# Head norms of a hybrid decoder trunk: squares split into a rounded high part and a remainder for the sum over a head

## The chip, the cores and the metric

The kernel runs on one core of one Trainium2 chip. The metric is device time in microseconds (us) of one execution. The profile is that of one profiled execution of the same kernel. In it PE is TensorE (matrix products; PEld its weight loads), DVE is VectorE, ACT is ScalarE, POOL is GpSimd and SP is SyncE, which issues transfers.

## The reference

Two layers of a decoder trunk, for 256 prompt tokens and 8 x 8 sample tokens (320 in all), width 2048. Each layer takes an RMS norm, one wide input projection, three token mixers (A: sliding-window attention, B: causal pooling, C: gated linear attention), gates, a branch projection, a merge and an output projection. The change is in branch A, in the norm of each query and key head:

```
def rms_norm(x, g):
    xf = x.astype(jnp.float32)
    y = xf * lax.rsqrt(jnp.mean(xf * xf, axis=-1, keepdims=True) + EPS)
    return (y * g.astype(jnp.float32)).astype(x.dtype)
...
    q = rope(rms_norm(a_q.reshape(bsz, L, A_HEADS, A_HEAD_DIM), q_norm_g), pos)
    k = rope(rms_norm(a_k.reshape(bsz, L, A_KV_HEADS, A_HEAD_DIM), k_norm_g), pos)
```

There are 16 query heads and 4 key heads of 64 numbers. With 64 numbers a head, 128 partitions hold two heads, and a tile of 128 x 2 x 320 holds four heads of all 320 tokens: one such tile for the keys (k_norm), four for the queries (q_norm 0 to 3), in each of the two layers.

## The kernel before, in words

Everything is held transposed: channels in partitions, the 320 tokens along the free dimension. The weights stream in from memory in blocks of 128 x 1024 float32, one block a "beat". Each block is split into a rounded high part `w_hi` (ACT, `split_hi`, L1108) and a remainder `w_lo` (DVE, `split_lo`, L449), both float32r, and PE forms three products for each 128 x 128 piece: high by high, high by low, low by high (`block_products`, through `mm`, L1554). That is 24 main products of 320 columns in a beat. There are 5 buffers of raw blocks and 3 of high parts, so ACT and DVE run up to a few beats ahead of PE, and are held back by `half_used`, which PE raises after each half block.

The other work on PE (norms, attention, linear attention) is cut into side steps. `side_steps` assigns each of them a beat, and PE does a beat's side steps behind the main products of that beat. ACT and DVE each have a list of their own, written out by beat too, and each engine goes through its list in order: in the loop over beats DVE does `split_lo_to(Q + 2)`, then, in beats with scores, `vector_softmax`, `split_lo_to(Q + 3)` and `vector_probs`, then `vector_part`, then `rope_end`. ACT does `split_hi_to(Q + 2)`, in beats with scores `split_hi_to(Q + 3)`, then `scalar_part`. Semaphores (`act_done`, `vec_done`, `step_done` and others) carry the dependences; a `mark` notes the value that a later `wait_mark` waits for.

A head norm runs like this. DVE takes the projected tile from the accumulators into `ta` (L518). ACT squares it into `tc` (L1353), for k_norm in beat 70 and for q_norm k in beat 77 + 4k. PE, at the end of beat 72 or 79 + 4k, multiplies `tc` by `head_ones`, a float32 block of ones for each head, which leaves each head's sum of squares in `side` banks 2 and 3. ACT takes the inverse root (L1128, L1130) into `tb`; DVE's `rope_pair` (L468, L792) scales and begins the rotation; SP exchanges halves by transfers (`turned<-normed`); DVE's `rope_end` ends the rotation, in beats 75, 81, 86, 90 and 94.

Scores step j stands on PE at the end of beat 82 + 4j for j of 0 to 2, and later for the others; `p_turn` two beats behind it and `pv` three. So in beats 82, 86 and 90 `scored_at` is true. `prompt_softmax` waits for the scores step of that beat, `prompt_probs` for the exponentials that ACT forms from it (L1279, L1281), and ends with four scalings of the probabilities (L837, L838).

The step on PE before:

```
elif name in ("k_norm", "q_norm"):
    wm("head_squares", l, (name, k))
    for t in range(2):
        last = mm(side[:, 2 + t, 0:TOK], head_ones, tc[:, t, :])
```

Of the kernel before, what the change touches and what calls it, by code (L numbers as in the profile page):

```python
# [17 lines left out]
F32 = mybir.dt.float32  # L18
F32R = mybir.dt.float32r
BF16 = mybir.dt.bfloat16  # L20
U8 = mybir.dt.uint8
ALU = mybir.AluOpType
ACT = mybir.ActivationFunctionType
AX = mybir.AxisListType

P = 128
# [7 lines left out]
TOK = SEQ + SMP  # L34
# [15 lines left out]
G_CQ, G_CK, G_CV, G_U, G_BZ, G_K, G_V, G_Q, G_CZ, G_AZ = 0, 2, 4, 8, 12, 16, 17, 18, 22, 26  # L50
# [103 lines left out]
STEP_NO = {s: i for i, s in enumerate(ORDER)}  # L154
N_STEPS = len(ORDER)

ROPE_END = {75: ("k_norm", 0), 81: ("q_norm", 0)}
ROPE_END.update({82 + 4 * k: ("q_norm", k) for k in range(1, 4)})

# [25 lines left out]
def gated_at(beat, stage):  # L185


    wait = {G_AZ: 2}
    return [g for g in GATED if TAKE[g] + wait.get(g, 0) + stage == beat and g != GATED[-1]]
# [16 lines left out]
def trunk(nc, ins, outs):  # L206
    with ExitStack() as ctx:
        def sem(name):
            return ctx.enter_context(nc.semaphore(name))
# [3 lines left out]
        def place(name, shape, dt=F32, at=None):  # L213

            size = {F32: 4, F32R: 4, BF16: 2, U8: 1}[dt]
            for s in shape[1:]:
                size *= s
            if at is None:
                at = top[0]
                top[0] += -(-size // 64) * 64  # L220
            return nc.alloc_sbuf_tensor_at(name, shape, dt, offset=at)
# [8 lines left out]
        T1 = TOK * 4  # L230

        part_b, part_c, part_a = br0, br0 + 16 * T1, br0 + 32 * T1
# [14 lines left out]
        near_mask = place("near_mask", [P, NEAR, 32], U8)  # L247
        par = place("par", [P, DEPTH, R_END])
        ones = place("ones", [P, P])
        eps = place("eps", [P, 1])  # L250
        rstd = place("rstd", [P, TOK])
        ta0 = top[0]
        ta = place("ta", [P, 2, TOK])
        tb = place("tb", [P, 2, TOK])
        tc = place("tc", [P, 2, TOK])
# [38 lines left out]
        v_stack = [place("v_stack0", [P, 1024], F32R), place("v_stack1", [P, 1024], F32R, at=att0)]  # L294
        squares = place("squares", [P, 4, TOK], at=part_c)
        w_gate = place("w_gate", [P, GH * DK], at=part_c + 12288 + 6144)
        turned = place("turned", [P, 2, TOK], at=part_c + 10 * T1)
        normed = place("normed", [P, 2, TOK], at=part_c + 12 * T1)
        cq = place("cq", [P, GH, TOK], at=part_a)
# [11 lines left out]
        side = ctx.enter_context(nc.psum_tensor("side", [P, 4, 512], F32))  # L311
# [18 lines left out]
        level_k = sem("level_k")  # L330
        softplus_done = sem("softplus_done")
        swapped = sem("swapped")
        params_in = sem("params_in")
        rms_done = sem("rms_done")
        x_hi_ready = sem("x_hi_ready")
# [18 lines left out]
        marks = {}  # L354

        def wait_mark(e, *key):
            s, v = marks[key]
            e.wait_ge(s, v)
# [31 lines left out]
        head_ones = const[:, C_BLOCK:C_BLOCK + P]  # L390
# [34 lines left out]
        def _(dve):  # L425
            v = Counted(dve, vec_done)
# [464 lines left out]
            def vector_part(l, beat):  # L891

                if l == 0:
                    for j in squares_at(beat):
                        first_squares(j)
                if l == 0 and beat == 10:
                    dve.wait_ge(consts_in, 64)
                    v(dve.tensor_copy(gmask[:, :, :], gmask_f[:, NEAR:8, :]))
                    for j in range(4):
                        rows = slice(32 * j, 32 * j + 32)  # L900
                        v(dve.tensor_copy(near_mask[rows, :, :], gmask_f[rows, 0:NEAR, rows]))
                    v(dve.memset(q_s[:, :, :, :, :, :].rearrange("p i b j g t -> p (i b j g t)"), 0.0))
                    v.mark("masks", 0, 0)
                if beat == RMS_BEAT:
                    from_act()
                if beat == LR_AT + 1:
                    for i in range(2 if l else 0):
                        dve.wait_ge(y_out[i], 64 * l)
                    dve.wait_ge(half_used, last_half(l, beat))
                    dve.tensor_tensor(ta[:, 0, :], group_psum(GROUPS * l + LR_GROUP)[:, 0, :], rstd[:, :],  # L910
                                      ALU.mult).then_inc(main_free, 1)
                    marks[("lr", l, 0)] = (main_free, GROUPS * l + LR_GROUP + 1)
                if beat == 12:
                    log_decay_sum(l)
                if beat == 13:
                    decay_scan(l)
                if beat == 15:
                    clear_scores(l)
                if beat == 14:

                    v(dve.memset(lev_k[:, :, :], 0.0))
                    v.mark("keys_clear", l, 0)
                for g in gated_at(beat, 2):
                    gate_low(l, g)
                for g in gated_at(beat, 1):
                    gate_product(l, g)
                if TAKEN_AT.get(beat, G_CZ) < G_CZ:
                    take(l, TAKEN_AT[beat])
                for gi in range(4):
                    if beat == TAKE[G_U + gi] + 1:  # L930
                        pool_diff(l, gi)
                for k in range(1, 8):
                    if beat == 17 + 2 * k:
                        level_prep(l, k)
                    if beat == 18 + 2 * k:
                        level_scale(l, k)
                for name, k, _ in STEPS.get(beat, ()):
                    if name == "gate":
                        log_decay(l)
                    elif name == "level":  # L940
                        (near_take if k < NEAR else level_take)(l, k)
                    elif name == "pool":
                        wait_step(l, "pool", k)
                        for t in range(2):
                            v(dve.tensor_scalar(o_ab[:, 2 * k + t, :], side[:, 2 + t, 0:TOK],
                                                col(l, R_PS + 2 * k + t), None, ALU.mult))
                        v.settle()
                        v.mark("pooled", l, k)
                    elif name == "second_chunk":
                        second_state(l)  # L950
                    elif name == "sample_gla":
                        sample_state(l, k)
                    elif name == "gla_norm":
                        gla_scale(l, k)
                    elif name in ("k_norm", "q_norm"):
                        rope_pair(l, name, k)
                if TAKEN_AT.get(beat, 0) >= G_CZ:

                    take(l, TAKEN_AT[beat])
                if beat == TAKE[GATED[-1]]:  # L960
                    gate_product(l, GATED[-1])
                    gate_low(l, GATED[-1])
                if beat == 34:
                    carry_prep(l)
                if beat == 36:
                    carry_end(l)
                if beat in STACK_AT:
                    stack_low(l, STACK_AT.index(beat))
                for k in range(8):
                    if beat == (SAMPLE_AT[k - 1] if k else 51):  # L970
                        sample_sel(l, k)
                if beat in (50, SAMPLE_AT[GH - 1]):
                    sample_queries(l, int(beat != 50))
                if beat in (68, 70):

                    from_act()
                    v(dve.tensor_tensor(squares[:, 0:4:2, :], squares[:, 0:4:2, :], squares[:, 1:4:2, :], ALU.add))
                    v.mark("squares", l, (beat - 68) // 2)
# [88 lines left out]
        def _(act):  # L1067
            a = Counted(act, act_done)
# [127 lines left out]
            def scalar_part(l, beat):  # L1196
# [119 lines left out]
                if beat in STACK_AT:  # L1316
                    n = STACK_AT.index(beat)
# [25 lines left out]
                for k in range(2):  # L1343
                    if beat == 68 + 2 * k:
# [1 line left out]
                        if k:  # L1346
                            wait_step(l, "gla_norm", 0)
                        give(act.activation(squares[:, :, :], o_c[:, 4 * k:4 * k + 4, :], ACT.Square))
                for name, k, at in [("k_norm", 0, 70)] + [("q_norm", k, 77 + 4 * k) for k in range(4)]:
                    if beat == at:  # L1350
                        s, n = marks[("taken", l, G_K if name == "k_norm" else G_Q + k)]
                        act.wait_ge(s, n)
                        a(act.activation(tc[:, :, :], ta[:, :, :], ACT.Square))  # L1353
                        a.mark("head_squares", l, (name, k))

            def mix_pair(l, j):
                Q0 = BEATS * l + IN_BEATS + 18 * j
# [157 lines left out]
        def _(pe):  # L1515
# [37 lines left out]
            def mm(out, lhsT, rhs, start=True, stop=True):  # L1553
                return pe.matmul(out, lhsT, rhs, start=start, stop=stop)  # L1554
# [31 lines left out]
            def side_step(l, name, k, banks):  # L1586
# [104 lines left out]
                    for i in range(2):  # L1691
                        last = mm(side[:, i, 0:TOK], ones[:, :], squares[:, 2 * i, :])
                elif name in ("k_norm", "q_norm"):
                    wm("head_squares", l, (name, k))
                    for t in range(2):
                        last = mm(side[:, 2 + t, 0:TOK], head_ones, tc[:, t, :])
                elif name == "kv_turn":
                    wm("taken", l, G_V)
                    for t in range(2):
# [247 lines left out]
```

## Time and profile before

| what | us |
|---|---|
| median of 3 runs | 2290.7 |
| lowest and highest of them | 2290.34, 2290.79 |
| the profiled execution, its own time | 2289.56 |
| its span, first to last instruction | 2287.8 |
| PE busy in the span | 2280.6 |
| DVE busy | 1357.3 |
| ACT busy | 968.9 |
| POOL busy | 70.8 |

The granted clock of TensorE is full in all 40 slices of the page. The rows below come from the page, from views of the trace that list waits and groups, from the chain of work that ended last (in order of time, merged by line, with the end of a piece where the next one starts), and from timelines of single engines. A matmul's record is longer than its place in the stream, since matmuls overlap: what one costs is read from the pieces of the chain.

### The profile page before, as it was taken

The page shows a single profiled execution, that of the slowest core. Times are in us where ns is not written, and L with a number is a line of the kernel's source. Part 1 is how long each engine was busy: PE and PEld are TensorE (multiplying, and loading weights), DVE is VectorE, ACT ScalarE, POOL GpSimd, SP SyncE. Part 2 cuts the span into 40 slices and gives each one's busy share as a digit, 9 for nine tenths or more (in the row PEclk, how much of TensorE's full clock was granted, in tenths as well). Part 3 has the DMA queues.
Part 4 walks back from the last instruction along what each step waited for, and adds up shares of the span by engine and source line. Part 5 has one row for each costly group of instructions (what it writes and reads, how often), then busy time and mean ns, then how long its engine had stood idle before and what let it go on. Part 6 is the DMA issues. An engine that isn't in the chain of part 4 may idle for free.

```text
span 2287.8 us, 40303 instructions
## 1 busy us (share of the span) xinstructions
PE 2280.6 (100%) x16664; PEld 2237.0 (98%) x16664; DVE 1357.3 (59%) x2414; ACT 968.9 (42%) x1762; POOL 70.8 (3%) x108
## 2 busy tenths in 40 slices
PE   9999999999999999999999999999999999999999
PEld 9999999999999999999999999999999999999999
DVE  6767757765455445446657777577654455545443
ACT  5444345544333333333344443456443333333332
POOL 0100100000000000000001001000000000000000
PEclk9999999999999999999999999999999999999999
DMA  7443654334444444445554436543344444444454
GB/s 277 149 153 130 228 191 137 117 122 153 150 148 149 153 149 148 149 153 196 188 209 138 149 129 240 183 142 111 127 148 152 153 148 148 152 152 148 148 198 152
DMA packets 99479, 364.06 MB, mean 159 GB/s; under 512 B 12048, under 2 KB 12304, under 8 KB 98464
## 3 DMA queue, kind: packets, MB, share of 16 engines
q1 hardware_dynamic: 88896, 317.76, 41.3%
q0 software_dynamic: 9680, 42.36, 5.2%
q8 instruction: 132, 2.16, 0.4%
q10 hardware_dynamic: 720, 1.36, 0.2%
q14 instruction: 51, 0.42, 0.1%
HBM read 341.59 MB, written 20.50 MB: 158 GB/s over the span
## 4 chain that ended last, share of the span: by engine, by line
PE 98%; DVE 1%; ACT 0%; issue 0%; DMA 0%; ACTq 0%; DVEq 0%
PE main L1554 91%; PE side L1554 6%; PE side L1558 1%; PE side L1753 0%; DMA par<-in_params 0%; PE side L1679 0%; DVE lev_e L705 0%; PE side L1760 0%; DVE lev_q L464 0%; DVE lev_k L712 0%; DVE w_lo L449 0%; ACT w_hi L1108 0%; ACT lev_e L1342 0%; PE side L1687 0%; DVE xg_lo L483 0%
## 5 line engine op out<-in xcount | busy, mean ns | idle before, releaser
L1554 PE MATMUL main<-xg_hi,w_hi 128*128 128x320 f32 x3488 | 1092.9, 313 | 0.7 <-DVE w_lo L449 0.6
L449 DVE TENSOR_TENSOR w_lo<-raw,w_hi 128x512 fp32r<-128x512 f32 x1192 | 791.4, 697 | 504.3 <-ACT w_hi L1108 498.5
L1554 PE MATMUL main<-xg_hi,w_lo 128*128 128x320 f32 x3488 | 1077.8, 309 | 0.0
L1554 PE MATMUL main<-xg_lo,w_hi 128*128 128x320 f32 x3488 | 1077.6, 309 | 0.0
L1108 ACT ACTIVATE w_hi<-raw 128x512 fp32r<-128x512 f32 x1192 | 716.8, 627 | 713.2 <-PE main L1554 693.8
L1554 PEld LDWEIGHTS main<-xg_hi,w_hi 128*128 128x128 f32 x3488 | 654.8, 188 | 9.9 <-issue 2.9
L1554 PEld LDWEIGHTS main<-xg_lo,w_hi 128*128 128x128 f32 x3488 | 655.0, 188 | 2.0
L1554 PEld LDWEIGHTS main<-xg_hi,w_lo 128*128 128x128 f32 x3488 | 654.7, 188 | 0.0
L1554 PE MATMUL main<-branch_hi,w_hi 128*128 128x320 f32 x768 | 237.3, 309 | 0.0
L1554 PE MATMUL main<-branch_lo,w_hi 128*128 128x320 f32 x768 | 237.3, 309 | 0.0
L1554 PE MATMUL main<-branch_hi,w_lo 128*128 128x320 f32 x768 | 237.3, 309 | 0.0
L1554 PE MATMUL main<-mg_hi,w_hi 128*128 128x320 f32 x512 | 158.2, 309 | 0.0
L1554 PE MATMUL main<-mg_lo,w_hi 128*128 128x320 f32 x512 | 158.2, 309 | 0.0
L1554 PE MATMUL main<-mg_hi,w_lo 128*128 128x320 f32 x512 | 158.2, 309 | 0.0
L1554 PEld LDWEIGHTS main<-branch_hi,w_hi 128*128 128x128 f32 x768 | 144.1, 188 | 0.0
L1554 PEld LDWEIGHTS main<-branch_lo,w_hi 128*128 128x128 f32 x768 | 144.1, 188 | 0.0
L1554 PEld LDWEIGHTS main<-branch_hi,w_lo 128*128 128x128 f32 x768 | 144.1, 188 | 0.0
L1364 ACT ACTIVATE tb<-ta 128x640 f32<-128x640 f32 x48 | 35.5, 740 | 174.0 <-DVE ta L989 174.0
L989 DVE TENSOR_TENSOR ta<-main,rstd 128x640 f32<-128x640 f32 x48 | 39.6, 825 | 100.6 <-PE main L1554 100.6
L1554 PEld LDWEIGHTS main<-mg_hi,w_hi 128*128 128x128 f32 x512 | 96.1, 188 | 0.0
L1554 PEld LDWEIGHTS main<-mg_lo,w_hi 128*128 128x128 f32 x512 | 96.1, 188 | 0.0
L1554 PEld LDWEIGHTS main<-mg_hi,w_lo 128*128 128x128 f32 x512 | 96.1, 188 | 0.0
(236 smaller groups left out, 1242.8 us busy)
## 6 DMA issues: line engine op xcount, KB each, us to landing
raw<-in_w_stream SPq DMA_DIRECT2D x595, 512.0 KB, 3.3
state<-in_state POOLq DMA_DIRECT2D x16, 512.0 KB, 6.1
out_state_s<-state POOLq DMA_DIRECT2D x16, 512.0 KB, 3.0
turned<-normed SPq DMA_DIRECT2D x40, 80.0 KB, 2.1
w_pool<-in_w_pool POOLq DMA_DIRECT2D x2, 1024.0 KB, 8.1
cache_k<-in_cache_k POOLq DMA_DIRECT2D x2, 1024.0 KB, 5.0
cache_v<-in_cache_v POOLq DMA_DIRECT2D x2, 1024.0 KB, 7.3
out_k_window<-in_cache_k_tok POOLq DMA_DIRECT2D x2, 960.0 KB, 9.9
```

The lines of the kernel that those rows point to most:

```text
L449: dve.tensor_tensor(w_lo[Q % RAWS][:, half], raw[Q % RAWS][:, half], w_hi[Q % HIS][:, half].bitcast(F32), ALU.subtract).then_inc(lo_ready, 1)
L989: dve.tensor_tensor(ta[:, :, :], group_psum(G0), two(rstd[:, :]), ALU.mult).then_inc(main_free, 1)
L1108: act.activation(w_hi[Q % HIS][:, half], raw[Q % RAWS][:, half], ACT.Copy).then_inc(hi_ready, 1)
L1364: give(act.activation(tb[:, :, :], ta[:, :, :], ACT.Sigmoid))
L1554: return pe.matmul(out, lhsT, rhs, start=start, stop=stop)
L1558: return pe.transpose(out, src, ident[0:src.shape[0], 0:src.shape[0]])
```

## The change

The squares go to PE as two float32r tiles instead of one float32 tile. ACT still squares `ta` into `tc`; it then waits for that and copies `tc` into `sq_hi`, which rounds it, and raises a new semaphore `squares_hi`. One beat later DVE, as the first thing after the masks and clears in `vector_part`, waits for that semaphore and subtracts: `sq_lo = tc - sq_hi`. PE waits for the subtraction instead of for the Square, and forms for each of the two halves two products with `head_ones_r`, a float32r copy of the block of ones made once in beat 10 of layer 0. The new tiles lie in memory of branch C that nothing uses at that time.

```diff
+SQUARES_AT = {70: ("k_norm", 0)}
+SQUARES_AT.update({77 + 4 * k: ("q_norm", k) for k in range(4)})
...
+        head_ones_r = place("head_ones_r", [P, P], F32R)
...
+        sq_hi = place("sq_hi", [P, 2, TOK], F32R, at=part_c + 4 * T1)
+        sq_lo = place("sq_lo", [P, 2, TOK], F32R, at=part_c + 6 * T1)
...
+        squares_hi = sem("squares_hi")
...
                     v(dve.memset(q_s[:, :, :, :, :, :].rearrange("p i b j g t -> p (i b j g t)"), 0.0))
+                    v(dve.tensor_copy(head_ones_r[:, :], head_ones))
                     v.mark("masks", 0, 0)
...
+                if beat - 1 in SQUARES_AT:
+                    dve.wait_ge(squares_hi, 5 * l + sorted(SQUARES_AT).index(beat - 1) + 1)
+                    v(dve.tensor_tensor(sq_lo[:, :, :], tc[:, :, :], sq_hi[:, :, :].bitcast(F32), ALU.subtract))
+                    v.mark("squares_low", l, SQUARES_AT[beat - 1])
                 for g in gated_at(beat, 2):
                     gate_low(l, g)
...
-                for name, k, at in [("k_norm", 0, 70)] + [("q_norm", k, 77 + 4 * k) for k in range(4)]:
-                    if beat == at:
-                        s, n = marks[("taken", l, G_K if name == "k_norm" else G_Q + k)]
-                        act.wait_ge(s, n)
-                        a(act.activation(tc[:, :, :], ta[:, :, :], ACT.Square))
-                        a.mark("head_squares", l, (name, k))
+                if beat in SQUARES_AT:
+                    name, k = SQUARES_AT[beat]
+                    wait_mark(act, "taken", l, G_K if name == "k_norm" else G_Q + k)
+                    a(act.activation(tc[:, :, :], ta[:, :, :], ACT.Square))
+                    a.settle()
+                    act.activation(sq_hi[:, :, :], tc[:, :, :], ACT.Copy).then_inc(squares_hi, 1)
...
                 elif name in ("k_norm", "q_norm"):
-                    wm("head_squares", l, (name, k))
+                    wm("squares_low", l, (name, k))
                     for t in range(2):
-                        last = mm(side[:, 2 + t, 0:TOK], head_ones, tc[:, t, :])
+                        mm(side[:, 2 + t, 0:TOK], head_ones_r[:, :], sq_hi[:, t, :], True, False)
+                        last = mm(side[:, 2 + t, 0:TOK], head_ones_r[:, :], sq_lo[:, t, :], False, True)
```

## Rows read from the trace of the kernel before

**Rows 1.** Page: busy time of each engine, share of the span, instructions.

```profile
PE 2280.6 (100%) x16664; PEld 2237.0 (98%) x16664; DVE 1357.3 (59%) x2414; ACT 968.9 (42%) x1762; POOL 70.8 (3%) x108
```

**Rows 2.** Page: the chain that ended last, shares of the span by engine, by line.

```profile
PE 98%; DVE 1%; ACT 0%; issue 0%; DMA 0%; ACTq 0%; DVEq 0%
PE main L1554 91%; PE side L1554 6%; PE side L1558 1%; PE side L1753 0%; DMA par<-in_params 0%; PE side L1679 0%; DVE lev_e L705 0%; PE side L1760 0%; DVE lev_q L464 0%; DVE lev_k L712 0%; DVE w_lo L449 0%; ACT w_hi L1108 0%; ACT lev_e L1342 0%; PE side L1687 0%; DVE xg_lo L483 0%
```

**Rows 3.** Waits of PE: waiter <- awaited: us in all, times, longest.

```profile
PE side L1554 <- DVE eps L473: 1.1, 1, 1.1
...
PE side L1554 <- ACT o_ab L1289: 0.9, 2, 0.4
PE main L1554 <- DVE w_lo L449: 0.6, 1, 0.6
PE side L1554 <- DVE q_s L803: 0.5, 1, 0.5
```

**Rows 4.** Groups of PE instructions by shape: count | busy us, mean ns | idle before.

```profile
L1554 PE MATMUL side<-tc,const 128*128 128x320 f32 x40 | 12.4, 431 | 0.0
```

**Rows 5.** Chain that ended last, layer 0, gla_norm and k_norm: start, us, what.

```profile
311.40 1.31 PE side L1554 x4
312.71 3.52 PE main L1554 x24
316.23 1.08 PE side L1554 x4
317.31 10.56 PE main L1554 x72
```

**Rows 6.** Timeline of ACT: start, us, line, out<-in, idle before: Square of q_norm 1.

```profile
351.62 0.74 ACT L1353 ACTIVATE tc<-ta 128x640 f32<-128x640 f32 x1 [3.69 <-DVE ta L518]
```

**Rows 7.** Groups of DVE instructions by line: subtractions with a float32r result.

```profile
L449 DVE TENSOR_TENSOR w_lo<-raw,w_hi 128x512 fp32r<-128x512 f32 x1192 | 791.4, 697 | 504.3 <-ACT w_hi L1108 498.5
...
L1003 DVE TENSOR_TENSOR mg_lo<-tc,mg_hi 128x640 fp32r<-128x640 f32 x16 | 13.2, 826 | 0.5
```

**Rows 8.** Timeline of DVE, layer 0, behind the masks of beat 10.

```profile
50.75 1.93 DVE L609 TENSOR_SCALAR lev_q<-side,par 128x320 f32<-128x320 f32 x4 [1.77 <-PE side L1554]
```

**Rows 9.** Timelines around q_norm 0, layer 0: ACT, DVE, then PE.

```profile
336.53 0.74 ACT L1353 ACTIVATE tc<-ta 128x640 f32<-128x640 f32 x1 [3.75 <-DVE ta L518]
...
337.89 2.65 DVE L449 TENSOR_TENSOR w_lo<-raw,w_hi 128x512 fp32r<-128x512 f32 x4 [1.39 <-ACT w_hi L1108]
...
342.44 1.24 PE L1554 MATMUL side<-tc,const 128*128 128x320 f32 x4
```

**Rows 10.** Timelines around gla_norm 1 and k_norm, layer 0: ACT and DVE.

```profile
309.26 0.72 ACT L1353 ACTIVATE tc<-ta 128x640 f32<-128x640 f32 x1
...
310.44 0.82 DVE L977 TENSOR_TENSOR squares<-squares 128x640 f32<-128x640 f32 x1
...
314.36 1.94 DVE L781 SCALAR_TENSOR_TENSOR o_c<-o_c,par,tb 128x320 f32<-128x320 f32 x4 [1.90 <-ACT tb L1130]
```

**Rows 11.** Timeline of DVE, layer 0: last scaling of the probabilities in beats 82, 86, 90.

```profile
360.37 0.28 DVE L838 TENSOR_SCALAR probs<-probs,small 128x128 f32<-128x128 f32 x1
...
378.11 0.28 DVE L838 TENSOR_SCALAR probs<-probs,small 128x128 f32<-128x128 f32 x1
378.43 0.83 DVE L464 TENSOR_TENSOR turned<-turned,const 128x640 f32<-128x640 f32 x1
...
395.98 0.28 DVE L838 TENSOR_SCALAR probs<-probs,small 128x128 f32<-128x128 f32 x1
```

**Rows 12.** Chain, layer 0: main work that follows q_norm 1, 2 and 3.

```profile
358.97 1.08 PE side L1554 x4
360.05 3.52 PE main L1554 x24
...
377.91 3.52 PE main L1554 x24
...
395.78 3.52 PE main L1554 x24
```

**Rows 13.** Layer 1, q_norm 1: last scaling on DVE (timeline), main work after it (chain).

```profile
1498.53 0.29 DVE L838 TENSOR_SCALAR probs<-probs,small 128x128 f32<-128x128 f32 x1
...
1498.23 3.52 PE main L1554 x24
```

## The prediction, made before the changed kernel was run

> **What bounds the kernel now.** I read three views in this order. First the busy shares of the page: TensorE (PE) is busy for 2280.6 of 2287.8 us, VectorE (DVE) for 59% and ScalarE (ACT) for 42% [rows 1]. Then the chain of work that ended last: 98% of it is PE, 91% the main weight stream and 6% side steps [rows 2]. Then what PE waits for: a handful of waits, the longest single one 1.1 us at the very start; those that belong to the attention stage are 0.9 us (two, for `o_ab`) and 0.5 us (one, for `q_s`) [rows 3]. So time taken out of PE's own stream is time saved one for one, and any idle time put into that stream is lost one for one. The other two engines count only where PE has to wait for them.
>
> **What the change takes from PE.** The ten head-norm steps (k_norm once and q_norm four times in each of 2 layers) are the 40 records of `side<-tc,const` [rows 4]: two float32 products a step, each recorded as two. What a step costs is read from the chain, not from the mean of a record, because records overlap: k_norm takes 1.08 us, between a beat of 24 main products in 3.52 us and 72 in 10.56 us [rows 5]. The main products are float32r, of 320 columns and full 128*128 weights, and both pieces give 0.147 us for one. The new step is four products of exactly that form: 4 x 0.147 = 0.587 us. Saved per step: 1.08 - 0.587 = 0.49 us; ten steps: 4.9 us. Bounds for one new product: 0.147 us (72 rows of the same form side by side) and 0.27 us (a quarter of the float32 step, the nearest other form); I take the first, since nothing but the source of the operands differs. The upper bound would take the whole 4.9 us back.
>
> The row of main products does not stand exactly where a rule would have it. The Trainium skill, "TensorE: Matmul & The Clock Gate", section "Back-to-back issue gap", gives columns / 2.4 + 2.5 ns for an isolated product, 135.8 ns for 320 columns by its formula, where the trace measures 147. By that figure the new step would be 0.543 us, an estimate from the page, and the sum 0.4 us lower. The trace has the same form 72 times in a row and decides.
>
> **What it adds beside PE.** ACT gets one Copy of 128x640 per step behind its Square. Nearest row: the Square itself, 0.74 us for the same tile [rows 6]. DVE gets one subtraction of 128x640 per step, and the same form exists in the kernel: `mg_lo` L1003, 0.825 us [rows 7]. Bounds: 0.70 us (the weight split, the same operation on 512 columns [rows 7]) and 0.87 us (that row scaled by 640 / 512). I take 0.83. One cast of 128 columns at beat 10 happens once; DVE idles 1.77 us just after that work [rows 8], so I cost it at nothing, and at some 0.2 us if that cover were gone.
>
> **What it moves: the release of PE.** Before, a head-norm step on PE needed only ACT's Square. Now it needs Square, then Copy, then DVE's subtraction. So the question is where in DVE's own order the subtraction stands. It is the first thing in `vector_part` of beats 71 and 78, 82, 86, 90; PE wants it at the end of beats 72 and 79, 83, 87, 91. But in beats 82, 86 and 90 `scored_at` is true, and there the DVE loop runs `vector_softmax`, a split, and `vector_probs` ahead of `vector_part`. That softmax waits for the scores step that PE does at the end of the same beat, one beat (3.7 us) ahead of the q_norm step. DVE runs its list in order.
>
> *Steps with room: k_norm and q_norm 0, 4 of 10.* At q_norm 0 ACT squares at 336.53, the Copy would end near 338.1, the weight copies behind it start 0.8 us later, DVE's two splits of the next beat end near 340.0, the subtraction near 340.9, and PE arrives at 342.44 [rows 9]: 1.5 us to spare. At k_norm the Square ends near 310.0 and the Copy near 310.8; the split behind it ends near 312.7 and the subtraction near 313.5, inside the 1.90 us in which DVE idled ahead of 314.36 [rows 10], and PE arrives at 316.2 [rows 5]. The cover of these is DVE's idle time; if it were gone, half a microsecond of lateness would eat the 0.49 us. I give each the full gain: 4 x 0.49 = 2.0 us.
>
> *Steps without room: q_norm 1, 2, 3, 6 of 10.* The Square is ready early (q_norm 1: 351.62 + 0.74 [rows 6]), and a Copy behind it too. But DVE is in the softmax of scores 0 and ends the last scaling of the probabilities only at 360.37 + 0.28 = 360.65; for q_norm 2 this end is 378.11 + 0.28 = 378.39, for q_norm 3 it is 396.26 [rows 11]. The next DVE instruction comes 0.04 us later (378.43). PE ended these steps at 360.05, 377.91 and 395.78, each 1.08 us after it had got there (q_norm 1: 358.97) [rows 12]. So the subtraction begins 1.7 us after PE got there. The end of the new step is worked out thus:
> - end of the probabilities + 0.04 + 0.83 for the subtraction: 361.52, 379.26, 397.13.
> - PE's start after a late release. The trace has one such case: at the second gla_norm step DVE's addition ends at 310.44 + 0.82 = 311.26 [rows 10], and PE's step (1.08 us when not late) ends at 311.40 + 1.31 = 312.71 [rows 5]. So the wake-up costs 312.71 - 1.08 - 311.26 = 0.37 us. Lower bound 0.14 us, from DVE's end to the chain's first product at 311.40; upper bound 0.6 us, the whole wait of the one late main product [rows 3], though that holds more than a wake-up. I take 0.37, since it is the same kind of step with tiles of the same size.
> - four products: 0.587.
> Ends: 362.48, 380.22, 398.09. Against before: +2.43, +2.31, +2.31 us. PE sits idle for about 2.5 to 2.7 us in each. Layer 1 repeats it: for its q_norm 1 the probabilities end at 1498.53 + 0.29 and the old step at 1498.23 [rows 13], the same +2.43; the other two stand alike there, so there are six. Sum: 2 x 2.43 + 4 x 2.31 = 14.1 us.
>
> Is the loss given back? What waits on PE (ACT's root, `rope_pair`, the next weights) keeps its distance to PE or gains. DVE's extra 0.83 us lies inside PE's wait. What is late next: `p_turn` needs the probabilities, which are ready before the subtraction. At most the 1.4 us of attention waits [rows 3] could vanish; I count none. ACT and SP's weight loads only get ahead, and the rope exchange on SP stays behind the same `normed`; POOL's transfers wait for nothing that moves here by more than this.
>
> **The sum.** -2.0 + 14.1 = +12.1 us. The profiled execution took 2289.56 us (span 2287.8), so it becomes 2301.7. The median of the runs is 2290.7, 1.1 us above the profiled one; on it the forecast is 2302.8 us, 0.53% slower. About 0.2% (4.6 us) is what a measurement of this kernel can tell from no change.
>
> **The rivals.**
> - *Only the gain shows.* If the subtraction reached DVE ahead of the softmax, or if the waiting on PE were hidden, all ten steps would give 0.49 us: 2290.7 - 4.9 = 2285.8. This is faster, just past the 0.2% line. The deciding point is the lateness: the six steps eat the gain of all ten once each ends 4.9 / 6 = 0.8 us later than it would with its product alone. For it: in four steps there is room, and PE is the bound. Against it: DVE's end of the probabilities is later than PE's arrival by 1.7 us already before the subtraction [rows 11, 12]. Chance 0.05.
> - *Float32r gives PE nothing* (the change doesn't do what it says: the new products at 0.27 us each). Then -4.9 is missing on all ten: +17.0, 2307.7. For it: the operands are other tiles than the main stream's. Against: the same form at 0.147 [rows 5]. Chance 0.04.
> - *The clock falls in the new gaps.* The granted clock is full in all 40 slices of before, and PE is never idle for over 1.1 us there [rows 3], so no row shows what a 2.6 us gap does. If each of six gaps were followed by one beat at half rate, that is 3.52 us [rows 5] more each, 21 us: 2323.9. The Trainium skill, "TensorE: Matmul & The Clock Gate", section "Why this matters for your kernels", warns of such gaps between bursts; no run so far shows it. Chance 0.05.
> - *Part is given back* by the waits that vanish, or the wake-up and subtraction are at their lower bounds: 1.4 + 6 x (0.23 + 0.13) = 3.6 us less, 2299.2. Chance of falling below 2299: 0.03.
>
> **How the numbers follow.** The forecast (the six waits as worked out, within the bounds of wake-up and subtraction) has 0.83. Upper end of its own terms: 6 x (0.23 + 0.04) = 1.6 us, 2304.4; the lower end is the last rival's, 2299.2. The range 2299 to 2308 reaches over the float32r rival and leaves out the clock, the gain alone and what lies lower still, about 0.13. Faster by over 0.2%: 0.03 (2285.8 lies only 0.3 us past the line); within 0.2%: 0.03; slower: 0.94.
>
> **What would show it.** Right: PE waits on DVE for the side steps of the head norms six times, 2.5 us each, on the new subtraction's line; four steps with no wait; the step in the chain about 0.59 us; main beats still 3.52 us; on DVE the subtraction standing directly behind the last scaling of the probabilities. Wrong: no such waits (rival one), four products taking 1.08 us (rival two), a granted clock under 1 after beat 83 (rival three), or waits on ACT's Copy instead.

## The result and the profile after

| what | before | after |
|---|---|---|
| median of 4 runs, us | 2290.54 | 2306.68 |
| lowest and highest, us | 2290.34, 2290.79 | 2305.03, 2307.47 |
| profiled execution, us | 2289.56 | 2305.03 |
| its span, us | 2287.8 | 2303.2 |
| its mean granted clock | 1.000 | 0.998 |

The changed kernel is slower: ratio 1.0070, 95% interval 1.0057 to 1.0083, so +16.1 us where +12.1 had been forecast. The time lies in the range given. Of all executions in this document one, of the kernel with the high part alone, fell into a slower state of the chip (2436.85 us at a mean clock of 0.851) and is left out of its median.

The page of the kernel after, its part on engines, the clock in 40 slices, and the chain that ended last, by engine (compare rows 1 and 2):

```profile
PE 2280.2 (99%) x16664; PEld 2238.8 (97%) x16664; DVE 1364.8 (59%) x2425; ACT 975.2 (42%) x1772; POOL 70.6 (3%) x108
...
PEclk9999999999999999999999999999999999999999
...
PE 96%; DVE 2%; ACT 1%; issue 0%; DMA 0%; ACTq 0%; DVEq 0%
```

PE's busy time is what it was, though it should have fallen by 4.9 us: records stretch when the clock falls, and it does, as will be seen. The chain now spends 3% on DVE and ACT instead of 1%. The clock line shows nothing; a slice is 58 us, and what happens lasts 3.

Who waited for whom, engine PE, after (compare rows 3):

```profile
PE side L1565 <- DVE sq_lo L932: 15.6, 6, 2.7
PE main L1565 <- DVE w_lo L455: 1.3, 1, 1.3
PE side L1565 <- DVE eps L479: 1.1, 1, 1.1
PE side L1569 <- DVE lev_k L718: 1.0, 2, 0.5
PE side L1565 <- ACT o_ab L1300: 0.8, 2, 0.4
```

One new line: six waits on the new subtraction, 2.6 us each, and no seventh. The chain of layer 0 after, start, us, what (compare rows 5 and 12):

```profile
312.59 3.52 PE main L1565 x24
316.11 0.58 PE side L1565 x4
316.69 10.56 PE main L1565 x72
...
341.99 0.58 PE side L1565 x4
342.57 7.06 PE main L1565 x48
...
360.56 0.83 PE side L1565 x4
361.38 3.52 PE main L1565 x24
...
380.74 0.82 PE side L1565 x4
381.56 3.52 PE main L1565 x24
...
400.91 1.41 PE side L1565 x4
402.32 4.25 PE main L1565 x24
```

k_norm (316.11) and q_norm 0 (341.99) take 0.58 us in place of 1.08. The end of q_norm 0 before, from the same view:

```profile
342.61 1.08 PE side L1554 x4
343.68 10.56 PE main L1554 x72
```

q_norm 1 ends at 361.38, 18.81 us behind q_norm 0 (342.57); before, the distance was 16.37 us (343.68 to 360.05), so +2.44. q_norm 2 comes 20.18 us behind that instead of 17.86: +2.32. The third takes 1.41 us, and the 24 main products behind it 4.25 instead of 3.52. At full clock the two pieces would be 0.82 and 3.52, as at q_norm 2: that is 1.3 us that the forecast's sum does not have. Busy time by stretch of the kernel after; the column behind POOL's is the granted clock:

```profile
395.00:401.00 6.00, 3.44 (x24) 3.20 (x23) 5.13 (x21) 1.96 (x9) 0.00 (x0) 0.95 0.47 165
401.00:402.00 1.00, 1.00 (x4) 1.00 (x5) 0.97 (x2) 0.00 (x0) 0.00 (x0) 0.50 0.02 8
402.00:403.00 1.00, 1.00 (x6) 1.00 (x5) 0.90 (x4) 0.64 (x1) 0.00 (x0) 0.50 0.00 0
403.00:404.00 1.00, 1.00 (x6) 1.00 (x5) 0.21 (x2) 0.97 (x3) 0.00 (x0) 0.60 0.00 0
404.00:405.00 1.00, 1.00 (x9) 1.00 (x8) 0.94 (x2) 0.96 (x2) 0.00 (x0) 1.00 0.07 16
```

The clock is at half (1.2 instead of 2.4 GHz) just as PE resumes, and returns at about 403.7. Ten products of that stretch come 0.27 us apart instead of 0.147. The same happened after q_norm 1 of layer 1 (1.3 us again), and once behind the gate step of layer 1, where there is no new wait and PE was busy throughout:

```profile
1194.00:1196.00 2.00, 2.00 (x8) 1.23 (x7) 0.25 (x1) 0.00 (x0) 0.00 (x0) 0.93 0.69 244
1196.00:1198.00 2.00, 2.00 (x9) 2.00 (x9) 1.68 (x4) 0.29 (x1) 0.00 (x0) 0.50 0.05 18
1198.00:1200.00 2.00, 2.00 (x12) 2.00 (x11) 0.00 (x0) 1.97 (x2) 0.00 (x0) 0.72 0.00 0
```

By the clock column these three rows lose 2 x (0.07 + 0.50 + 0.28) = 1.7 us. Without the three falls this execution would have taken 2305.03 - 2 x 1.3 - 1.7 = 2300.7 us, an estimate.

That DVE's list makes the wait is read from its timeline around q_norm 2, after (start, us, line):

```profile
378.32 0.16 DVE L470 TENSOR_TENSOR small<-small 128x4 f32<-128x4 f32 x1 [0.70 <-ACT small L1292]
...
379.45 0.28 DVE L844 TENSOR_SCALAR probs<-probs,small 128x128 f32<-128x128 f32 x1
379.77 0.83 DVE L932 TENSOR_TENSOR sq_lo<-tc,sq_hi 128x640 fp32r<-128x640 f32 x1
380.51 0.82 DVE L470 TENSOR_TENSOR turned<-turned,const 128x640 f32<-128x640 f32 x1
```

The subtraction stands right behind the last scaling, ends at 380.60, and PE resumes at 380.74.

### The profile page after: what moved, and what is told of

It is laid out like the page before. It is cut to its first block, busy times and chain, and to the rows that moved or that the text cites. A ratio compares the mean times of both kernels' runs of the same rounds, so it can differ in the third digit from the quotient of the medians.

```text
span 2303.2 us, 40324 instructions
## 1 busy us (share of the span) xinstructions
PE 2280.2 (99%) x16664; PEld 2238.8 (97%) x16664; DVE 1364.8 (59%) x2425; ACT 975.2 (42%) x1772; POOL 70.6 (3%) x108
## 4 chain that ended last, share of the span: by engine, by line
PE 96%; DVE 2%; ACT 1%; issue 0%; DMA 0%; ACTq 0%; DVEq 0%
PE main L1565 90%; PE side L1565 5%; PE side L1569 1%; ACT probs L1290 0%; DVE w_lo L455 0%; DVE probs L823 0%; DVE sq_lo L932 0%; PE side L1765 0%; DMA par<-in_params 0%; PE side L1690 0%; DVE lev_e L711 0%; DVE probs L825 0%; PE side L1772 0%; DVE lev_q L470 0%; DVE lev_k L718 0%
```

## The experiments

My theory has two parts: (1) the six waits come only from the place of the subtraction in DVE's list, and are worth 14.1 us against 4.9 us of gain from the products; (2) the excess over that, 4 us, is the clock, which falls in some of the new gaps. (As the rows above show, of the 4.3 us lost to the clock in the profiled execution 2.6 belong to gaps; the other 1.7 belong to a place that the change did not touch.) The rivals were that the chain over two engines is too long in itself, that the float32r products cost more than they seem to, and that the excess lies elsewhere.

The runs of one kernel differ by up to 4 us, and the mean granted clock goes with it: the slower runs of the kernel before have 0.998 or 0.999. So beside the medians I compare the fastest execution whose mean clock is 1.000, where there is one. For the kernel before that is 2288.99 us in the first comparison and 2289.28 in the second. The means of all executions at 1.000, instead of the fastest, give the same differences within 0.1 us.

**The subtraction ahead of the softmax.**

```diff
                     split_lo_to(Q + 2)
+                    squares_low(l, beat)
                     if scored_at(beat):
                         vector_softmax(l, beat)
```

`squares_low` holds the wait and the subtraction, which are gone from `vector_part`.

> Edit: the changed kernel with DVE's subtraction moved ahead of the softmax, to the place right behind the first split of the beat; nothing else. My theory (the six waits come only from the subtraction standing behind softmax and probabilities in DVE's list): all six waits of PE on sq_lo vanish, the ten steps each keep 0.58 us, the granted clock is 1.000, and the time is 2290.5 - 4.9 = 2285.6 us. The softmax of beats 82 starts up to 0.9 us later, which p_turn's 2 us of room take up. Rival (the chain Square, Copy, subtraction over two engines is itself too long): waits of PE on sq_lo stay in some steps and the time is above 2290 us.

Measured: 2286.64 us median of 11 runs against 2290.66 of 21; ratio 0.9981 (0.9972 to 0.9990). At clock 1.000: 2284.12, 4.9 us under before. No wait on `sq_lo`. DVE and then the chain of this kernel:

```profile
353.20 1.29 DVE L455 TENSOR_TENSOR w_lo<-raw,w_hi 128x512 fp32r<-128x512 f32 x2
354.41 0.82 DVE L900 TENSOR_TENSOR sq_lo<-tc,sq_hi 128x640 fp32r<-128x640 f32 x1
355.14 0.48 DVE L823 CUSTOM_DVE_ANT_0 probs<-side,amask_p,par 128x256 f32<-128x256 f32 x1
```

```profile
357.94 0.58 PE side L1568 x4
358.52 3.53 PE main L1568 x24
```

The subtraction is over at 355.2, 2.7 us ahead of PE, and the softmax behind it is about 0.8 us later, which nobody notices. The median gained 4.0 us and not 4.9; the full-clock executions differ by just the forecast's product term. Executions of both kernels lose a varying part to the clock: I had expected 1.000, and nine of the 11 have 0.999. In the profiled one the clock fell once, behind the gate step of layer 1. This shows part (1), and it is a version faster than both kernels.

**The waits alone.** PE forms the old float32 products, and still waits for the subtraction.

```diff
-                        mm(side[:, 2 + t, 0:TOK], head_ones_r[:, :], sq_hi[:, t, :], True, False)
-                        last = mm(side[:, 2 + t, 0:TOK], head_ones_r[:, :], sq_lo[:, t, :], False, True)
+                        last = mm(side[:, 2 + t, 0:TOK], head_ones, tc[:, t, :])
```

> Edit: the changed kernel, but PE forms the two float32 products with tc as before; Copy, subtraction and the wait on it stay. The remainder is computed and not used. My theory: the waits alone cost 2 x 2.92 + 4 x 2.80 = 17.0 us with no gain from the products, so 2307.5 us, and 1.3 us more for each gap after which the clock falls: 2308 to 2312, mean clock 0.996 to 0.999. Rival (the float32r products themselves are what costs): about 2290.5 us.

Measured: 2310.41 us (2307.53 to 2313.46), ratio 1.0088 (1.0072 to 1.0103), mean clock 0.996 to 0.999. As expected, but for a highest run 1.5 us above my 2312: the loss is in the wait, the products are a gain. It lies 3.7 us above the changed kernel, where the product term is 4.9 and either kernel's executions spread over 2 us or more.

**Between softmax and probabilities.**

```diff
                         vector_softmax(l, beat)
                         split_lo_to(Q + 3)
+                        squares_low(l, beat)
                         vector_probs(l, beat)
```

In beats without scores the subtraction stays where the changed kernel has it.

> Edit: the changed kernel with the subtraction between vector_softmax with its split and vector_probs, so ahead of the wait for ACT's exponentials. My theory: PE's waits shrink to about 0.4 us each, since the subtraction now ends near 1.1 us earlier than the old release plus nothing of the probabilities: +0.32 us for q_norm 1 and +0.19 us for q_norm 2 and 3, so 1.4 us of loss against 2.0 us of gain, 2290.0 us, within 0.2% of before; no gap is long, so the clock stays 1.000. Rival (any late release costs a fixed amount whatever its length): near 2300 us.

Measured: 2288.85 us, ratio 0.9990 (0.9982 to 0.9999); at clock 1.000 2287.68, 1.3 us under before. PE's waits of this kernel:

```profile
PE side L1570 <- DVE small L470: 2.2, 6, 0.4
```

Six waits are left, of 0.4 us. (They are put down to a DVE line beside the subtraction.) The loss is shorter by about 0.1 us a step than I worked out, hence -1.3 and not -0.5. The cost follows the lateness, not the number of waits. Five of the 11 runs have a mean clock of 1.000 and six 0.999, where I had expected 1.000; in the profiled one the single fall stands behind the gate step of layer 0, and none at the six waits.

**The gap filled with products.**

```diff
+                    if name == "q_norm" and k:
+                        for _ in range(16):
+                            mm(side[:, 2, 0:TOK], head_ones_r[:, :], xg_hi[:, 0, :])
                     wm("squares_low", l, (name, k))
```

> Edit: the changed kernel, with 16 float32r products of 320 columns (2.35 us) into a bank that the step then overwrites, on PE ahead of the wait in q_norm 1, 2 and 3. They only fill the time in which PE was idle. Theory that the part of the loss beyond the forecast (some 2.6 us in the profiled run) is the clock falling to half in some of the gaps: the granted clock is 1.000 in every run, the spread of the runs shrinks from 2.4 us to under 0.6 us, and the time is 2302.3 to 2303. Rival (the extra is something else, in DVE or the weight stream): 2305 to 2307.5 as in the changed kernel.

Measured: 2301.25 us median (2300.90 to 2302.40), ratio 1.0047 (1.0033 to 1.0060). Three of its four executions have clock 1.000, the fourth 0.999. PE does useless work in place of idling (the wait on `sq_lo` is 0.5 us in all, in two steps), and DVE releases it as late as in the changed kernel, yet it is 5.4 us faster than the changed kernel. Granted clock, in the stretches of the waits:

```profile
355.00:361.00 6.00, 5.91 (x40) 5.64 (x39) 5.13 (x21) 1.96 (x9) 0.00 (x0) 1.00 0.45 152
...
375.00:381.00 6.00, 6.00 (x42) 5.87 (x40) 5.00 (x20) 1.96 (x9) 0.00 (x0) 1.00 0.44 150
...
401.00:405.00 4.00, 3.86 (x26) 3.61 (x25) 3.67 (x9) 2.58 (x4) 0.00 (x0) 1.00 0.12 48
```

In its profile the clock falls nowhere. At full clock it stands 11.9 us above before: this is the forecast's sum of 12.1, and the rest of the changed kernel's loss is the clock. It is not quite the changed kernel at full clock: from the end of the subtraction to the end of the first late step it takes 0.92 us where the changed kernel takes 0.98, some 0.4 us over the six. It ended 1 us below the 2302.3 that I expected, because I had added 12 us to the median of before, which holds lost clock, and not to its full-clock time. Its spread is 1.5 us and not under 0.6, with one run at 0.999. Part of the 5.4 us may be falls that failed to come behind the gate step, which nothing in the edit touches: why it shows so few of those, four runs cannot tell.

**The changed kernel again, and the gap made longer.** The second of these does the subtraction twice:

```diff
+                    for _ in range(2):
                         v(dve.tensor_tensor(sq_lo[:, :, :], tc[:, :, :], sq_hi[:, :, :].bitcast(F32), ALU.subtract))
+                        v.settle()
```

> The changed kernel itself, unedited, more often and beside its variants. If the forecast's +12.1 us is right for executions whose clock never falls, the lowest time lies near 2289.0 (lowest of before) + 12 = 2301 us only if one execution keeps its full clock, and each fall adds about 1.3 us: times between 2301 and 2309, higher where the mean granted clock is lower. If the extra is not the clock, the times do not follow the clock column and never come under 2304.

> Edit: DVE does the subtraction twice, the second behind the first, so PE waits 0.86 us longer in six steps and idles for about 3.5 us in each. My theory: lowest time 6 x 0.86 = 5.2 us above the changed kernel at full clock (2301 + 5.2 = 2306 us); if a longer gap lets the clock fall more often, up to all six gaps, 1.3 us each or more: 2306 to 2316 and a mean clock at or under 0.997. Rival (the gap's length does not matter for the clock): median 5.2 us above the changed kernel's median in the same comparison, same clock.

Measured, unedited: 2306.77 us (2305.74 to 2309.40), ratio 1.0072 (1.0060 to 1.0085), all at clock 0.996 to 0.998, the slowest at the lowest. None kept its full clock, and none came under 2304, which I had named as a sign against the clock; but the times follow the clock column. Its profile has two falls in the new gaps (1.4 and 1.3 us) and two behind the gate steps (1.7 each): 2307.19 less these is 2301.0, an estimate like the 2300.7 above. So the 2301 of the forecast was not measured in the changed kernel itself, only in the one with the filled gap. Doubled: 2321.84 us, ratio 1.0138 (1.0124 to 1.0152), clock 0.991 to 0.993. That is 15.1 us above the changed kernel for 5.2 us of longer waiting; the rest, 9.9 us, came with the lower clock, more than I had allowed for (2306 to 2316). Its chain, layer 0:

```profile
361.70 0.82 PE side L1567 x4
362.52 5.05 PE main L1567 x24
...
384.27 1.41 PE side L1567 x4
385.67 5.61 PE main L1567 x24
...
407.98 1.41 PE side L1567 x4
409.38 5.68 PE main L1567 x24
```

Now each gap is followed by a fall (layer 1 alike: 5.05, 5.56, 5.66 for 24 products), and it lasts longer: 1.5 to 2.8 us lost each time, 13.8 in all, where the 2.6 us gaps of the changed kernel lost 1.3 or 1.4. The profiled 2320.86 less 13.8 is 2307.1, near the 2306 worked out for a full clock.

**The high part alone.** The subtraction and its product are left out; PE waits for ACT's Copy.

```diff
-                    wm("squares_low", l, (name, k))
+                    pe.wait_ge(squares_hi, 5 * l + (0 if name == "k_norm" else 1 + k) + 1)
                     for t in range(2):
-                        mm(side[:, 2 + t, 0:TOK], head_ones_r[:, :], sq_hi[:, t, :], True, False)
-                        last = mm(side[:, 2 + t, 0:TOK], head_ones_r[:, :], sq_lo[:, t, :], False, True)
+                        last = mm(side[:, 2 + t, 0:TOK], head_ones_r[:, :], sq_hi[:, t, :])
```

> Edit: the remainder is left out: no subtraction, one float32r product per half with the rounded squares, and PE waits for ACT's Copy only. It leaves out the low part of the squares, so the sums are less exact. My theory: no waits, a step of 2 x 0.147 = 0.29 us instead of 1.08, so 10 x 0.79 = 7.9 us less than before: 2281.1 at full clock, about 2282.7 as median. Rival (a step has a fixed cost beside its products, or ACT's Copy is late): less than 7 us of gain, with waits on ACT.

Measured: 2282.00 us, the median of five (2281.36 to 2283.11), ratio 0.9962 (0.9949 to 0.9975); at clock 1.000 2281.36, 7.9 us under before. The chain has a step of two products:

```profile
358.09 0.29 PE side L1561 x2
358.38 3.52 PE main L1561 x24
```

So a step costs its products at 0.147 us and nothing else, and ACT's Copy is never late.

**The subtraction on POOL.**

```diff
+                def squares_low(n):
+                    pool.wait_ge(squares_hi, 5 * l + n + 1)
+                    pool.tensor_tensor(sq_lo[:, :, :], tc[:, :, :], sq_hi[:, :, :].bitcast(F32),
+                                       ALU.subtract).then_inc(squares_lo, 1)
```

DVE's wait and subtraction are gone, and PE waits for `squares_lo`.

> Edit: the subtraction runs on POOL instead of DVE, in POOL's own list, with a semaphore of its own. POOL's product of the same size takes 1.86 us before. My theory (only DVE's order makes the waits): POOL is free in beats 78 to 91, the subtraction ends 1.9 us after the Copy, ahead of PE in all ten steps: no waits, the same gain as with the subtraction moved ahead on DVE, 4.9 us under before: about 2285.7. Rival (POOL's pass is too slow, or slows DVE while both run): PE waits on POOL, time at or above before.

Measured: 2287.45 us (2287.04 to 2290.05), ratio 0.9987 (0.9978 to 0.9996); at clock 1.000 2287.04, only 2.2 us under before. There is no wait on POOL, but PE's waits have this line:

```profile
PE side L1570 <- DVE q_s L810: 3.2, 2, 1.8
```

and the timelines of DVE and POOL, layer 0, show why:

```profile
351.67 0.82 DVE L471 TENSOR_TENSOR q_a<-q_a,turned 128x640 f32<-128x640 f32 x1
352.53 2.13 DVE L810 COPY q_s<-q_a 64x64 f32<-64x64 f32 x4
```

```profile
352.40 1.56 POOL L1491 TENSOR_TENSOR sq_lo<-tc,sq_hi 128x640 fp32r<-128x640 f32 x1 [13.02 <-ACT sq_hi L1362]
```

The four small copies into `q_s` took 0.85 us before and take 2.13 us here. It is the first of them that is long, 1.47 us instead of 0.19, and it ends when POOL's pass does (352.40 + 1.56 = 353.96); the other three take 0.18 to 0.20 us. They release scores 0, for which PE already waited 0.5 us before [rows 3]; it is now 3.2 us over both layers (1.4 and 1.8). These 2.7 us are what is missing from 4.9. Part (1) holds (the ten steps are released in time), and the rival was right in its second half.

The same pattern stands beside all ten of POOL's passes in this trace: one instruction of DVE is drawn out beyond the pass's end. In two of them it is the first copy, which ends within 0.1 us of the pass; in the other eight it is a weight split, of 1.58 to 1.90 us instead of 0.70, which ends some 0.5 us behind the pass and for which PE did not wait. That POOL holds DVE up is read from this coincidence, ten times of ten; no run takes it apart.

The profiled execution, 2288.90 us, also has one fall of the clock. It comes after the 1.8 us wait of layer 1: the 24 main products behind it take 5.24 us instead of 3.71. After the 1.4 us wait of layer 0 there was none.

## Why the prediction was right, and where its size was off

- *PE is the bound, and products cost 0.147 us.* Right: 0.58 us a step for four, 0.29 for two. The product term of 4.9 us is what the early subtraction gave at full clock. The estimate from the Trainium skill, "TensorE: Matmul & The Clock Gate", section "Back-to-back issue gap", 0.543 us, was too low, as the rows of before had said.
- *Four steps with room.* Right. DVE idled 1.90 us ahead of the norm products at k_norm before, and 1.03 us after.
- *Six steps without room.* Right in place, cause and size: +2.44 and +2.32 us measured, +2.43 and +2.31 worked out. From the subtraction's end (359.58 + 0.82 = 360.40) to the step's end (361.38) is 0.98 us, against 0.37 + 0.587 = 0.96. Moving one instruction removed all six waits.
- *The sum.* 12.1 us forecast; 11.9 us at full clock, with the gaps filled.
- *The range.* That the time lies in it is partly luck. The terms of the forecast, each at its upper bound, end at 2304.4 us, and all four runs are above that (lowest 2305.03), so what I had given a chance of 0.83 did not happen. The range went up to 2308 to take in the rival on float32r products, which was false; the clock, which did add the time, had been left out of it.
- *The clock.* Here the forecast failed, by 4 us. The step that failed is the rival on the clock: it had the mechanism, but I gave it a chance of 0.05 and made it all or none, six falls of 3.5 us. The sign that I had named for it, a granted clock under 1 after beat 83, is in the profile. In truth it falls in some gaps and not in others, with 1.3 us for each, because it comes back within ten products. Not all of the loss is in the gaps either: the falls behind the gate step cost the changed kernel 1.7 us in one profile and 3.4 in the other. The kernel before loses to the clock too, 1.6 us from its full-clock time to its median, and I had taken that as it stood. The argument against the rival, "the granted clock is full in all 40 slices of before", was weak twice. The slices are too coarse: the page of after has the same row of nines. And one execution is not all: the profiled one of before kept its clock, others of it have a mean of 0.998 or 0.999 and take up to 2293 us. The Trainium skill, "TensorE: Matmul & The Clock Gate", section "Why this matters for your kernels", warned of idle gaps between bursts of products. The runs agree that gaps matter, but they show falls after gaps shorter than that section speaks of: 2.6 us, where a fall came in five of 18 cases, and 1.8 us.
- *The rivals.* Only the gain: false for the change as made, true once the subtraction is moved. No gain from float32r: false. Given back later: the `q_s` wait is missing in the profiled execution of after, but its repeat has it at 0.7 us. PE's waits outside the six add up to 4.1 us before and to 4.2 and 3.8 in these two, so at most 0.3 us was given back.

## What to carry over

An operand's new step has to be looked for in the list of the engine that does it, and not by the engine's load: DVE was 59% busy, but the instruction stood behind a wait for PE's own later work. Put work that releases the bounding engine ahead of any wait in that list. Where the bounding engine is TensorE, price an idle gap above its length, and look at the mean clock of all runs before taking one profile as typical.

## What the runs showed of the hardware

- After an idle gap of PE of 2.6 us the clock stood at half in two of six cases of the first profile, for some 3 us, at 1.3 us each; the profile of its repeat has two of six as well, and that of the waits alone one of six. After gaps of 3.5 us it did so in six of six, at 1.5 to 2.8 us each. After the two gaps of the POOL run it did so once: after 1.8 us, at 1.5 us, and not after 1.4. With gaps of 0.4 us, or with the gap filled by products, it did not in the profiles taken.
- The clock also falls where PE never waits: in the main products behind the gate step (whose products have 16 rows), at 1.7 us each, in the profiles of the changed kernel, its repeat, the early subtraction, the waits alone and the subtraction between softmax and probabilities, but not in the other five, that of before among them. No profile of the kernel before shows such a fall; that they make its spread of 4 us is inferred from its clock column. Why they come in some executions and not in others stays open.
- Beside a 128x640 pass of POOL, one DVE instruction was drawn out until the pass was over (copies) or some 0.5 us longer (splits), in ten passes of ten: a 64x64 copy took 1.43 and 1.47 us instead of 0.19, a 128x512 split 1.58 to 1.90 instead of 0.70.
